# The output projection by pairs of token tiles, seven half-size products for eight, with sums on GpSimd

## The chip, the cores and the metric

The kernel runs on one core of a Trainium2 chip. The metric is the device time of one execution in microseconds. All arithmetic is fp32.

## The reference, cut to what matters

Two layers of an encoder run over 1152 token rows: 1024 of a prompt, and 8 x 16 of samples. Three branches (RWKV-7, latent attention, stick-breaking attention) each give 512 channels a row. At the end of a layer they are merged, projected and added to the residual:

```python
merged = (gA * ((yA * jax.nn.silu(zA)) @ P['w_br_rwkv'][l])
          + gB * ((yB * jax.nn.silu(zB)) @ P['w_br_mla'][l])
          + gC * ((yC * jax.nn.silu(zC)) @ P['w_br_sb'][l]))
x = x + gate * (merged @ P['w_out'][l])      # (1152 x 1024) @ (1024 x 1024)
```

The change touches the last line: `merged @ w_out`, and how its result gets into x.

## The kernel before

Each layer is a row of stages with a barrier between two (`Stages.stage`, line 116). The last one is `merge`. Each engine has its own program in it, and semaphores tie them together.

**Units.** 24 units (token half tp, branch b, pair of column blocks m) make the merged activations `M` (`mergedT`: channels on the partitions, 8 blocks x 1152 tokens). A unit is 14 products: 7 of the gate projection (four matmul steps of 288 columns each) and 7 of the branch projection (two steps each). Each group of 7 does a 2 x 2 block product by the scheme with seven multiplications, for which sums of blocks are made first: `quarter_sums` on GpSimd for the weights (line 2412), lines 2512 to 2515 on GpSimd for y, `h_sum` on VectorE for the normed input hT. ScalarE copies a partial bank (`kept`), VectorE adds it to another (`added`), and TensorE waits for the copy before it goes on accumulating in the same bank. VectorE adds each quarter to `M` and counts `merged`, one a unit.

**Output projection (lines 2571 to 2584).** `ups` lists 18 products: column half n of w_out, and token tile i of nine, half 0 first. Each is 8 matmul steps (128 x 128 weights from `M`, 512 columns of w_out) into one of four banks. The first two may start while VectorE ends the last unit, since they read only tokens of the first half; the third waits for `tanh_done`, and the fifth for all of `merged`. Each reuse of a bank waits for `update_read`. The halves of w_out lie where hT was (`w_half`); the second is loaded as the last unit's gate products end (line 2486).

**Update (lines 2660 to 2666).** For each product VectorE multiplies the bank by `gate` into t, tells `update_read`, and adds t to one of four x tiles. SP (the queue that issues DMAs) stores the tile, and loads the x tile for the update three places ahead into the one that came free. `InOrder` (line 94) makes an engine wait for the end of each of its own operations before the next. GpSimd has nothing to do in the stage once it has made the sums of the last unit.

Of the kernel before, what the change touches and what calls it, by code (L numbers as in the profile page):

```python
# [8 lines left out]
ALU = mybir.AluOpType  # L9
# [4 lines left out]
P = 128  # L14
D = 1024
KD = D // P
# [6 lines left out]
NT = T // P  # L23
# [2397 lines left out]
def merge(nc, S, A, l, ps, con, hT, yg, gates, x_in, x_out, wg0, wgs0):  # L2421
# [4 lines left out]
             "products", "kept", "tanh_done", "added", "quarter_read", "merged", "w_out0_loaded", "w_out1_loaded", "gate_loaded",  # L2426
             "x0_moved", "x1_moved", "x2_moved", "x3_moved", "updates", "update_read", "updated", "vec", "pool_own")
    with S.stage(*names) as (block, sb, (y0_loaded, y1_loaded, wg0_loaded, wg1_loaded, wb0_loaded, wb1_loaded, gate_sums, branch_sums, y_sums, h_sums,
                                         products, kept, tanh_done, added, quarter_read, merged, w_out0_loaded, w_out1_loaded, gate_loaded,
                                         x0_moved, x1_moved, x2_moved, x3_moved, updates, update_read, updated, vec, pool_own)):  # L2430
        M = sb("mergedT", [P, KD, T])
# [17 lines left out]
        NU, PER_Y = len(units), KD // 2  # L2449
        ups = [(n, i) for n in range(2) for i in range(NT)]  # L2450

# [45 lines left out]
        def _(pool):  # L2497
# [3 lines left out]
            for u in range(NU):  # L2501
# [15 lines left out]
                quarter_sums(G, own, wb[u % 2], wbs[u % 2], HP // 2, branch_sums)  # L2517

        @block.tensor
        def _(pe):  # L2520
# [49 lines left out]

            banks = (6, 7, 0, 1)
            pe.wait_ge(merged, NU // 2)
            for j, (n, i) in enumerate(ups):
                if i == 0:
                    pe.wait_ge(w_out_loaded[n], 16)
                if j == 2:
                    pe.wait_ge(tanh_done, 4 * NU)
                if j == 4:
                    pe.wait_ge(merged, NU)
                if j >= 4:  # L2580
                    pe.wait_ge(update_read, j - 3)
                for k in range(KD):
                    last = mm(ps[:, banks[j % 4], :], M[:, k, P * i:P * i + P], w_half(n)[:, k, :], start=(k == 0), stop=(k == KD - 1))  # L2583
                last.then_inc(updates, 1)

        @block.scalar
        def _(act):
# [10 lines left out]
            for u in range(NU):  # L2598
                keep(u, 1, gk[:, 0, :], 0)
                keep(u, 3, gk[:, 1, :], 0)  # L2600
                tanh(u, 0)
                keep(u, 4, gk[:, 2, :], 2)
                tanh(u, 1)
                tanh(u, 2)
                act.wait_ge(products, 14 * u + 7)
                if u >= 1:
                    act.wait_ge(quarter_read, u)
                do(gq[:, 3, :], ps[:, 0, 0:TQ], ACT.Tanh, scale=0.5).then_inc(tanh_done, 1)
                if u >= 1:
                    act.wait_ge(added, 6 * u)  # L2610
                keep(u, 8, bk[:, 0, :], 3)
                keep(u, 10, bk[:, 1, :], 3)
                keep(u, 11, bk[:, 2, :], 5)

        @block.vector
        def _(dve):
# [43 lines left out]
            put = InOrder(dve, updated)  # L2660
            for j, (n, i) in enumerate(ups):
                dve.wait_ge(updates, j + 1)
                dve.wait_ge(x_moved[j % 4], 16 * (2 * (j // 4) + 1))
                put(V.tensor_tensor(t[j % 2][:, :], ps[:, (6, 7, 0, 1)[j % 4], :], gate[:, int(i == NPT), 512 * n:512 * n + 512], ALU.mult))
                V.engine_nop().then_inc(update_read, 1)
                put(V.tensor_tensor(x[j % 4][:, :], x[j % 4][:, :], t[j % 2][:, :], ALU.add))


# [94 lines left out]
```

## Time and profile before

| | |
|---|---|
| median of 3 runs | 4752.07 us (4747.45 to 4758.35) |
| profiled execution | 4753.94 us, its span 4752.1 us |
| TensorE (PE) busy | 4376.5 us, 92% of the span |
| VectorE (DVE) busy | 2227.1 us, 47% |
| ScalarE (ACT) busy | 1628.7 us, 34% |
| GpSimd (POOL) busy | 731.5 us, 15% |
| line 2583, output projection, TensorE busy | 247.5 us in 576 records, for both layers |
| mean granted clock of TensorE | 0.969 of full speed |

The span runs from the first to the last instruction of one execution. Busy shares are means over stages with different limits, so what a stage is bound by is read in its own stretch. PE stands for matmuls, PEld for weight loads, which lie beside matmuls. The output projection of layer 0 lies from 2258.8 to 2382.5 us, that of layer 1 from 4623.9 to 4747.6 us. An fp32 matmul leaves two records in the trace.

### The profile page before, as it was taken

The numbers are of one execution on the slowest core, as the hardware profiler recorded it, in microseconds if no ns is written. First come the engines' busy times: TensorE is split into PE (matmuls) and PEld (weight loads), VectorE is DVE, ScalarE is ACT, GpSimd is POOL, SyncE is SP. The second block draws the span as 40 slices with busy tenths as digits, with TensorE's granted clock in tenths as the row PEclk, the third lists the DMA queues.
The fourth block names the chain that finished last, engine by engine and source line by source line (L and its number), as shares of the span: only waits on it lengthen the run. The fifth ranks groups of instructions, "written<-read, shape, count | busy, mean of one in ns | idle before, by whom it ended". The sixth has DMA issues, their size and how long they took to land. (4 is left out here: it accounts for less than half of the span.)

```text
span 4752.1 us, 74863 instructions
## 1 busy us (share of the span) xinstructions
PE 4376.5 (92%) x29552; PEld 3029.9 (64%) x29552; DVE 2227.1 (47%) x4660; ACT 1628.7 (34%) x3862; POOL 731.5 (15%) x940
## 2 busy tenths in 40 slices
PE   7899997988989989999979999979898999899999
PEld 3656665667666667777446666646666566677774
DVE  2555664345524453534225656633455244544341
ACT  4333333345523342112043333334455244411210
POOL 0011010000010015543000110000000100245430
PEclk9999998999999999999989999989999999999999
DMA  5010112010021122322241210120100211223222
GB/s 193 23 34 10 26 29 78 21 35 14 12 86 56 53 74 83 115 88 75 75 189 23 34 15 26 25 86 13 35 16 10 86 57 56 74 90 107 87 80 71
DMA packets 150654, 280.78 MB, mean 59 GB/s; under 512 B 51545, under 2 KB 77401, under 8 KB 145058
## 3 DMA queue, kind: packets, MB, share of 16 engines
q1 hardware_dynamic: 150306, 275.99, 18.2%
q8 instruction: 237, 3.88, 0.4%
q14 instruction: 111, 0.91, 0.1%
HBM read 230.96 MB, written 42.62 MB: 58 GB/s over the span
## 5 line engine op out<-in xcount | busy, mean ns | idle before, releaser
L1054 PE MATMUL banks<-hT,w_piece 128*128 128x384 f32 x1536 | 547.6, 498 | 6.3 <-ACT raw L1158 6.0
L1054 PEld LDWEIGHTS banks<-hT,w_piece 128*128 128x128 f32 x1536 | 280.6, 194 | 175.3 <-issue 14.0
L2232 PE MATMUL banks<-hT,w_piece 128*128 128x384 f32 x1056 | 354.1, 489 | 1.4 <-ACT sb_gate_raw L2342 1.4
L2232 PEld LDWEIGHTS banks<-hT,w_piece 128*128 128x128 f32 x1056 | 196.1, 190 | 141.4 <-issue 16.6
L2583 PE MATMUL banks<-hT,mergedT 128*128 128x512 f32 x576 | 247.5, 592 | 0.0
L1998 DVE SCALAR_TENSOR_TENSOR keysT<-banks,gains,rstd 64x128 f32<-64x128 f32 (+1 forms) x272 | 112.1, 412 | 249.1 <-ACT rstd L1912 246.6
L2592 ACT ACTIVATE gate_kept<-banks 128x288 f32<-128x288 f32 x144 | 59.0, 410 | 433.1 <-PE banks L2524 433.1
L2629 DVE TENSOR_TENSOR gate_quarters<-gate_kept,banks 128x288 f32<-128x288 f32 x144 | 65.4, 454 | 302.7 <-PE banks L2524 297.7
L2583 PEld LDWEIGHTS banks<-hT,mergedT 128*128 128x128 f32 x576 | 109.4, 190 | 137.0 <-issue 136.8
L2404 DVE TENSOR_TENSOR_SCAN left<-pass,zero 128x384 f32<-128x384 f32 (+7 forms) x144 | 189.8, 1318 | 5.0
L2629 DVE TENSOR_TENSOR branch_quarters<-branch_kept,banks 128x288 f32<-128x288 f32 x144 | 65.5, 455 | 270.3 <-PE banks L2524 270.3
L2401 DVE TENSOR_TENSOR pass<-pass,constants 128x128 f32<-128x128 f32 x128 | 41.5, 324 | 310.8 <-ACT take L2353 308.3
L1015 POOL TENSOR_TENSOR state_decayed<-state,decay_of_chunk 128x128 f32<-128x128 f32 x120 | 85.9, 716 | 572.7 <-DVE state L1287 568.9
L2524 PE MATMUL banks<-hT,w_gate_ahead 128*128 128x288 f32 x576 | 151.9, 415 | 7.4 <-PEq L132 7.4
L1830 PE MATMUL banks<-keysT,queriesT 96*128 96x512 f32 (+3 forms) x384 | 148.8, 496 | 8.7 <-DVE queriesT L1998 8.7
L2524 PE MATMUL banks<-y_branch,w_branch 128*128 128x288 f32 x576 | 155.3, 406 | 0.0
L2524 PE MATMUL banks<-hT,w_gate 128*128 128x288 f32 x576 | 147.5, 406 | 0.0
L2524 PEld LDWEIGHTS banks<-hT,w_gate_ahead 128*128 128x128 f32 x576 | 111.8, 195 | 40.0 <-issue 8.8
L1928 ACT ACTIVATE exponentials<-banks,maximum 128x384 f32<-128x384 f32 (+4 forms) x144 | 104.1, 723 | 92.8 <-DVE maximum L2011 91.2
L2229 PE MATMUL banks<-w_piece,hT 128*128 128x128 f32 x1152 | 132.7, 276 | 0.0
L1939 ACT ACTIVATE exponentialsT<-banks 128x512 f32<-128x512 f32 (+3 forms) x208 | 94.9, 488 | 105.3 <-PE banks L1842 104.7
L2229 PEld LDWEIGHTS banks<-w_piece,hT 128*128 128x128 f32 x1152 | 130.2, 192 | 1.0
(395 smaller groups left out, 9445.4 us busy)
## 6 DMA issues: line engine op xcount, KB each, us to landing
w_piece<-in_w_cols SPq DMA_DIRECT2D x66, 512.0 KB, 4.4
w_ada<-in_w_ada SPq DMA_DIRECT2D x24, 1024.0 KB, 9.4
w_gate_ahead<-in_w_cols SPq DMA_DIRECT2D x48, 512.0 KB, 4.3
w_branch<-in_w_br SPq DMA_DIRECT2D x96, 256.0 KB, 2.9
w_gate<-in_w_cols SPq DMA_DIRECT2D x48, 512.0 KB, 4.3
y_branch<-y_gated SPq DMA_DIRECT2D x12, 1152.0 KB, 8.2
sb_cached_keysT<-in_sbkT SPq DMA_DIRECT2D x8, 1024.0 KB, 6.9
sb_cached_values<-in_sbv SPq DMA_DIRECT2D x8, 1024.0 KB, 5.2
```

Source lines behind the costliest of these rows:

```text
L1015: G.tensor_tensor(SD[:, :], ST[:, :], R.pend[h % 2][:, n + 1:n + 2].broadcast_to([P, P]), ALU.mult).then_inc(sd_made, 1)
L1054: last = mm(dst, w[0 if kind in ("k", "v") else 1][:, k, :], hT[:, k, c], start=(k == 0), stop=(k == KD - 1))
L1830: last = mm(ps[:, b0 + a // 512, 0:e - a], Q[hh][:, P * i:P * i + P], K[hh][:, a:e], start=True, stop=True)
L1928: do(E[u % 3][:, 0:width(u)], sbank(u)[:, 0:width(u)], ACT.Exp, bias=mx[:, u:u + 1], scale=scale, accum_out=rsum[:, u:u + 1]).then_inc(exp ...
L1939: do(ET[:, s % 4, units[u][3], 0:cnt, :].rearrange("p q n -> p (q n)"), ps[:, ring_bank(("t", u, g)), 0:P * cnt], Copy).then_inc(ring_free, 1)
L1998: ins = V.scalar_tensor_tensor(to[hh][0:64, c], ps[hc, bank[n], at], par[hc, gain:gain + 1], rs[x % 2][hc, at], ALU.mult, ALU.mult)
L2229: last = mm(ps[:, bank[n], P * q:P * q + P], hT[:, k, P * i:P * i + P], w_of[wn][:, k, :], start=(k == 0), stop=(k == KD - 1))
L2232: last = mm(ps[:, bank[n], 0:TG], w_of[wn][:, k, :], hT[:, k, TG * g:TG * g + TG], start=(k == 0), stop=(k == KD - 1))
L2404: own(V.tensor_tensor_scan(mine[:, 0:n][:, ::-1], G[k][:, 0:n][:, ::-1], zero[:, 0:1].broadcast_to([P, n]), 1.0, ALU.mult, ALU.add))
L2524: ins = mm(ps[:, bank, 0:TQ], w[:, k, :], b[:, k, :], start=(first and k == 0), stop=(k == half - 1), skip_group_check=True)
L2583: last = mm(ps[:, banks[j % 4], :], M[:, k, P * i:P * i + P], w_half(n)[:, k, :], start=(k == 0), stop=(k == KD - 1))
L2629: own(V.tensor_tensor(dst, src, ps[:, bank, 0:TQ], ALU.add), added)
```

## The change

Two products stay as they were, for token tile 0: (0,0) and (1,0), eight steps each, one for each half of w_out. The other eight token tiles are taken in four pairs (`row_pair`). For a pair the rows are cut in two (one tile each), the inner dimension in two (4 blocks of 128 each), and the columns in two (512 each). The 2 x 2 block product is made in 7 products of four steps where there were 8, in the order of the units above.

The sums that it needs are made on GpSimd. For w_out there are four operations once a layer on [128, 4 x 512] elements: three go into buffers that the last units leave (`BS`: y_branch0, w_gate_ahead and w_gate1), and one over b12 in place, once the two whole products have read it (`updates` 2). For the pairs there is `quarter_sums` on [128, 4 x 128] elements, four operations a pair, into the buffers of the gate weights' sums and over a21 in `M`. ScalarE copies three partial banks a pair into the y_branch1 buffer (`ok`). VectorE adds them to a bank into t, and then multiplies and adds as before; the fourth update of a pair comes straight from its bank. Pairs take banks 0 to 2 and 3 to 5 in turn. Both halves of w_out are now needed for the first two products, and all of `merged` for the third. The order of the updates (`ups`), and with it that of the x tiles, is new. The semaphore names in the stage's list change with it: update_read goes, and out_products, out_kept, out_added, out_row_sums and out_sums come.

```diff
@@ -2447,7 +2447,14 @@
         w_out_loaded, x_moved = (w_out0_loaded, w_out1_loaded), (x0_moved, x1_moved, x2_moved, x3_moved)
         units = [(tp, b, m) for tp in range(2) for b in range(3) for m in range(KD // 2)]
         NU, PER_Y = len(units), KD // 2
-        ups = [(n, i) for n in range(2) for i in range(NT)]
+        NX = NPT // 2
+        ups = [(0, 0), (1, 0), *(u for x in range(NX) for u in ((0, 2 * x + 1), (1, 2 * x + 2), (1, 2 * x + 1), (0, 2 * x + 2)))]
+        wide = lambda ap, pattern: ap.rearrange(pattern)[:, 0:4 * 512].rearrange("p (k n) -> p k n", k=4)
+        BS = [wide(Y[0][:, :, :], "p h t -> p (h t)"), wide(wg[0][:, :, :, :], "p q k n -> p (q k n)"), wide(wg[1][:, :, :, :], "p q k n -> p (q k n)")]
+        ok = Y[1][:, :, :].rearrange("p h t -> p (h t)")[:, 0:3 * 512].rearrange("p (j n) -> p j n", j=3)
+
+        def row_pair(x):
+            return M[:, :, P * (2 * x + 1):P * (2 * x + 3)].rearrange("p k (q n) -> p q k n", q=2)
 
         def cols(tp, q):
             return slice(THALF * tp + TQ * q, THALF * tp + TQ * q + TQ)
@@ -2516,6 +2523,26 @@
                 pool.wait_ge(wb_loaded[u % 2], 32 * (u // 2 + 1))
                 quarter_sums(G, own, wb[u % 2], wbs[u % 2], HP // 2, branch_sums)
 
+            def row_sums(x):
+                if x >= 2:
+                    pool.wait_ge(out_products, 7 * (x - 1))
+                quarter_sums(G, own, row_pair(x), wgs[x % 2], KD // 2, out_row_sums)
+
+            pool.wait_ge(merged, NU // 2)
+            pool.wait_ge(products, 14 * (NU - 1) + 7)
+            row_sums(0)
+            for n in range(2):
+                pool.wait_ge(w_out_loaded[n], 16)
+            b11, b12, b21, b22 = (w_half(j)[:, KD // 2 * i:KD // 2 * i + KD // 2, :] for i in range(2) for j in range(2))
+            own(G.tensor_tensor(BS[0], b12, b11, ALU.subtract))
+            own(G.tensor_tensor(BS[1], b22, BS[0], ALU.subtract), out_sums)
+            own(G.tensor_tensor(BS[2], b21, BS[1], ALU.subtract))
+            pool.wait_ge(updates, 2)
+            own(G.tensor_tensor(b12, b22, b12, ALU.subtract), out_sums)
+            pool.wait_ge(merged, NU)
+            for x in range(1, NX):
+                row_sums(x)
+
         @block.tensor
         def _(pe):
             def product(bank, w, b, first, last):
@@ -2568,20 +2595,40 @@
                 pe.wait_ge(added, 6 * u + 5)
                 product(3, w[:, 1, half:HP], Ys[:, 2], False, True)
 
-            banks = (6, 7, 0, 1)
             pe.wait_ge(merged, NU // 2)
-            for j, (n, i) in enumerate(ups):
-                if i == 0:
-                    pe.wait_ge(w_out_loaded[n], 16)
-                if j == 2:
-                    pe.wait_ge(tanh_done, 4 * NU)
-                if j == 4:
+            for n in range(2):
+                pe.wait_ge(w_out_loaded[n], 16)
+                for k in range(KD):
+                    last = mm(ps[:, 6 + n, :], M[:, k, 0:P], w_half(n)[:, k, :], start=(k == 0), stop=(k == KD - 1))
+                last.then_inc(updates, 1)
+
+            def out_product(bank, w, b, first, last):
+                for k in range(KD // 2):
+                    ins = mm(ps[:, bank, :], w[:, k, :], b[:, k, :], start=(first and k == 0), stop=(k == KD // 2 - 1), skip_group_check=True)
+                ins.then_inc(out_products, 1)
+
+            half = KD // 2
+            b11, b12, b21, b22 = (w_half(j)[:, half * i:half * i + half, :] for i in range(2) for j in range(2))
+            for x in range(NX):
+                w, s, b0 = row_pair(x), wgs[x % 2], 3 * (x % 2)
+                if x == 0:
                     pe.wait_ge(merged, NU)
-                if j >= 4:
-                    pe.wait_ge(update_read, j - 3)
-                for k in range(KD):
-                    last = mm(ps[:, banks[j % 4], :], M[:, k, P * i:P * i + P], w_half(n)[:, k, :], start=(k == 0), stop=(k == KD - 1))
-                last.then_inc(updates, 1)
+                if x >= 2:
+                    pe.wait_ge(out_added, 4 * (x - 1))
+                out_product(b0, w[:, 0, 0:half], b11, True, False)
+                out_product(b0 + 1, w[:, 0, half:KD], b21, True, True)
+                pe.wait_ge(out_row_sums, x + 1)
+                pe.wait_ge(out_sums, 1)
+                pe.wait_ge(out_kept, 3 * x + 1)
+                out_product(b0, s[:, 1], BS[1], False, False)
+                out_product(b0 + 2, s[:, 0], BS[0], True, False)
+                pe.wait_ge(out_sums, 2)
+                pe.wait_ge(out_kept, 3 * x + 2)
+                out_product(b0, w[:, 1, 0:half], b12, False, False)
+                pe.wait_ge(out_kept, 3 * x + 3)
+                out_product(b0 + 2, s[:, 2], b22, False, True)
+                pe.wait_ge(out_added, 4 * x + 2)
+                out_product(b0, w[:, 1, half:KD], BS[2], False, True)
 
         @block.scalar
         def _(act):
@@ -2611,6 +2658,18 @@
                 keep(u, 8, bk[:, 0, :], 3)
                 keep(u, 10, bk[:, 1, :], 3)
                 keep(u, 11, bk[:, 2, :], 5)
+
+            def out_keep(x, n, j, read):
+                act.wait_ge(out_products, 7 * x + n)
+                if x >= 1:
+                    act.wait_ge(out_added, 4 * (x - 1) + read)
+                do(ok[:, j, :], ps[:, 3 * (x % 2) + (0, 0, 2)[j], :], ACT.Copy).then_inc(out_kept, 1)
+
+            act.wait_ge(products, 14 * NU)
+            for x in range(NX):
+                out_keep(x, 1, 0, 1)
+                out_keep(x, 3, 1, 3)
+                out_keep(x, 4, 2, 2)
 
         @block.vector
         def _(dve):
@@ -2658,12 +2717,26 @@
             dve.wait_ge(gate_loaded, 16)
             own(V.tensor_scalar(gate[:, :, :], gate[:, :, :], 0.5, None, ALU.mult))
             put = InOrder(dve, updated)
-            for j, (n, i) in enumerate(ups):
-                dve.wait_ge(updates, j + 1)
+
+            def update(j, source, read=None):
+                n, i = ups[j]
+                put(V.tensor_tensor(t[j % 2][:, :], source, gate[:, int(i == NPT), 512 * n:512 * n + 512], ALU.mult))
+                if read is not None:
+                    own(V.engine_nop(), read)
                 dve.wait_ge(x_moved[j % 4], 16 * (2 * (j // 4) + 1))
-                put(V.tensor_tensor(t[j % 2][:, :], ps[:, (6, 7, 0, 1)[j % 4], :], gate[:, int(i == NPT), 512 * n:512 * n + 512], ALU.mult))
-                V.engine_nop().then_inc(update_read, 1)
                 put(V.tensor_tensor(x[j % 4][:, :], x[j % 4][:, :], t[j % 2][:, :], ALU.add))
+
+            for n in range(2):
+                dve.wait_ge(updates, n + 1)
+                update(n, ps[:, 6 + n, :])
+            for x_ in range(NX):
+                for j, (n, kept_n, slot, bank) in enumerate(((2, 1, 0, 1), (5, 3, 2, 0), (6, 2, 1, 2))):
+                    dve.wait_ge(out_products, 7 * x_ + n)
+                    dve.wait_ge(out_kept, 3 * x_ + kept_n)
+                    own(V.tensor_tensor(t[j % 2][:, :], ok[:, slot, :], ps[:, 3 * (x_ % 2) + bank, :], ALU.add), out_added)
+                    update(2 + 4 * x_ + j, t[j % 2][:, :])
+                dve.wait_ge(out_products, 7 * x_ + 7)
+                update(2 + 4 * x_ + 3, ps[:, 3 * (x_ % 2), :], out_added)
 
 
 def pieces(w):
```

## Rows read from the trace of the kernel before

**Rows 1.** the page: span, and busy time of TensorE (its share is in brackets)

```profile
span 4752.1 us, 74863 instructions
...
PE 4376.5 (92%) x29552; PEld 3029.9 (64%) x29552; DVE 2227.1 (47%) x4660; ACT 1628.7 (34%) x3862; POOL 731.5 (15%) x940
```

**Rows 2.** chain that ended last, in order of time: start us, us, what, times

```profile
4579.89 44.13 PE banks L2524 x182
4624.03 123.61 PE banks L2583 x288
```

**Rows 3.** the page's costliest groups: busy, mean ns of one, idle before

```profile
L2583 PE MATMUL banks<-hT,mergedT 128*128 128x512 f32 x576 | 247.5, 592 | 0.0
...
L2583 PEld LDWEIGHTS banks<-hT,mergedT 128*128 128x128 f32 x576 | 109.4, 190 | 137.0 <-issue 136.8
```

**Rows 4.** line 2583 by stretch: us, PE, PEld busy, granted clock, DMA, GB/s

```profile
2258.76:2382.52 123.76, 123.76 (x288) 54.53 (x287) 1.00 0.21 69
4623.86:4747.60 123.74, 123.73 (x288) 54.53 (x287) 1.00 0.21 70
```

**Rows 5.** instructions in order of time, layer 0: start us, us, engine, line

```profile
2250.03 2.10 PE L2524 MATMUL banks<-h_sums,w_gate 128*128 128x288 f32 x8
...
2251.97 2.10 PE L2524 MATMUL banks<-y_branch,w_branch 128*128 128x288 f32 x8
...
2252.16 0.60 SPq L2486 DMA_DIRECT2D hT<-in_w_out  x1
...
2258.76 123.76 PE L2583 MATMUL banks<-hT,mergedT 128*128 128x512 f32 x288
```

**Rows 6.** line 2486: both loads of the second half of w_out, issue to landing

```profile
DMA to landing us min/median/max: 8.5/8.8/9.1
```

**Rows 7.** instructions in order of time, layer 1: load, first output product

```profile
4617.27 0.60 SPq L2486 DMA_DIRECT2D hT<-in_w_out  x1
...
4623.86 4.46 PE L2583 MATMUL banks<-hT,mergedT 128*128 128x512 f32 x10
```

**Rows 8.** GpSimd by line: duration ns min/median/max, first and last start

```profile
L2415 POOL TENSOR_TENSOR w_gate_sums_ahead<-w_gate_ahead x24: 1261/1268/1273, 1403.4 to 4561.1; 128x512 f32<-128x512 f32 x24
...
L1011 POOL TENSOR_TENSOR silu_z<-silu_z,temp x8: 2616/2618/2630, 228.2 to 3093.7; 128x1152 f32<-128x1152 f32 x8
...
L1020 POOL TENSOR_TENSOR bonus<-r_shifted,v_transposed x8: 2989/2996/3090, 151.4 to 3019.6; 128x1152 f32<-128x1152 f32 x8
```

**Rows 9.** instructions in order of time: VectorE beside GpSimd's sums, layer 0

```profile
2156.50 1.27 POOL L2416 TENSOR_TENSOR w_gate_sums_ahead<-w_gate_sums_ahead,w_gate_ahead 128x512 f32<-128x512 f32 x1
...
2156.68 1.40 DVE L2638 SCALAR_TENSOR_TENSOR gate_quarters<-gate_quarters,branch_quarters 128x288 f32<-128x288 f32 x1
...
2157.85 1.37 POOL L2417 TENSOR_TENSOR w_gate_ahead<-w_gate_ahead 128x512 f32<-128x512 f32 x1
...
2158.12 1.42 DVE L2639 TENSOR_TENSOR mergedT<-mergedT,gate_quarters 128x288 f32<-128x288 f32 x1
```

**Rows 10.** instructions in order of time: VectorE around the first output product

```profile
2254.65 0.46 DVE L2638 SCALAR_TENSOR_TENSOR gate_quarters<-gate_quarters,branch_quarters 128x288 f32<-128x288 f32 x1
...
2257.07 0.45 DVE L2629 TENSOR_TENSOR branch_quarters<-branch_kept,banks 128x288 f32<-128x288 f32 x1 [1.47 <-PE banks L2524]
...
2260.99 0.46 DVE L2639 TENSOR_TENSOR mergedT<-mergedT,gate_quarters 128x288 f32<-128x288 f32 x1
...
2261.49 1.22 DVE L2659 TENSOR_SCALAR gate<-gate 128x2048 f32<-128x2048 f32 x1
```

**Rows 11.** groups of instructions: copies of 512 columns, and the update's multiplication

```profile
L1939 ACT ACTIVATE exponentialsT<-banks 128x512 f32<-128x512 f32 x96 | 55.6, 596 | 82.5 <-PE banks L1842 82.5
...
L2664 DVE TENSOR_TENSOR update<-banks,gate 128x512 f32<-128x512 f32 x18 | 12.5, 692 | 95.7 <-PE banks L2583 95.7
```

**Rows 12.** DMA issues, layer 0's projection: KB each, median us to landing

```profile
x_rows<-in_x_prompt SPq DMA_DIRECT2D x12, 256.0 KB, 3.0
```

**Rows 13.** by stretch: us, busy PE, PEld, DVE, ACT, POOL, clock, DMA, GB/s

```profile
2382.60:2400.00 17.40, 0.00 (x0) 0.00 (x0) 1.61 (x4) 5.63 (x9) 0.00 (x0) 0.56 0.71 271
```

More of the change, by code:

```diff
@@ L2426, in merge @@
              "products", "kept", "tanh_done", "added", "quarter_read", "merged", "w_out0_loaded", "w_out1_loaded", "gate_loaded",
-             "x0_moved", "x1_moved", "x2_moved", "x3_moved", "updates", "update_read", "updated", "vec", "pool_own")
+             "x0_moved", "x1_moved", "x2_moved", "x3_moved", "updates", "updated", "out_products", "out_kept", "out_added", "out_row_sums", "out_sums", "vec", "pool_own")
     with S.stage(*names) as (block, sb, (y0_loaded, y1_loaded, wg0_loaded, wg1_loaded, wb0_loaded, wb1_loaded, gate_sums, branch_sums, y_sums, h_sums,
                                          products, kept, tanh_done, added, quarter_read, merged, w_out0_loaded, w_out1_loaded, gate_loaded,
-                                         x0_moved, x1_moved, x2_moved, x3_moved, updates, update_read, updated, vec, pool_own)):
+                                         x0_moved, x1_moved, x2_moved, x3_moved, updates, updated, out_products, out_kept, out_added, out_row_sums, out_sums, vec, pool_own)):
         M = sb("mergedT", [P, KD, T])
```

## The prediction

> **What bounds the kernel now.** I read the page first: TensorE is busy for 92% of the span, and no other engine for more than half of that share [rows 1]. An average says nothing of one stage, so the chain that ended last comes next. It shows that in the last stretch the matmuls of line 2524 run into those of line 2583 without a gap, and that line 2583 then holds the chain for 123.6 us, until the last residual update [rows 2]. The group of line 2583 has no idle time ahead of it [rows 3], and its two stretches, one for each layer, are 123.76 and 123.74 us of PE busy without a hole, at a granted clock of 1.00, the upper of the two levels (2.4 GHz) [rows 4]. So the output projection costs what its matmuls cost, and nothing else in that stretch sets its end. The next layer begins behind a barrier, and so what is saved in layer 0 moves all that follows.
>
> **What is removed.** A layer has 18 products (nine tiles, two column halves) of eight steps: 144 matmuls. In the trace each is two records, 288 a layer. 123.76 us / 144 = 0.859 us for a matmul [rows 4]. After the change it is 2 products of eight steps and 4 pairs x 7 products x 4 steps: 16 + 112 = 128 matmuls. Sixteen fewer, of the same shape (128 rows of weights, 512 columns): 16 x 0.859 = 13.75 us a layer, 27.5 us in all. All of it lies on the path.
>
> **Shorter products.** The new products wait between each four steps, where the old ones waited between each eight. The gate products of line 2524 have this form (four steps, semaphores between, accumulation into a bank that ScalarE copies meanwhile). One takes 1.94 us from its start to that of the next (2250.03 to 2251.97) [rows 5], which is 242.5 ns a record at 288 columns. A record at 512 columns takes 123.76 / 288 = 429.7 ns. The difference, 187.2 ns for 224 columns, is 0.836 ns a column, two cycles at 2.4 GHz (0.833), so nothing is left over. So a boundary whose waits are already met costs nothing that shows: I take 0. The upper bound is one exposed weight load, 0.19 us [rows 3], at each of 28 boundaries: 5.3 us a layer.
>
> **When the operands are needed (layer 0).** The first output product starts at 2258.76 [rows 5]. With 0.859 us a matmul: product (0,0) ends at 2265.6, (1,0) at 2272.5. Then the seven of pair 0, 3.44 us each, end at 2275.9, 2279.4, 2282.8, 2286.3, 2289.7, 2293.1, 2296.6. So the second half of w_out is needed at 2265.6 (before: only after nine tiles), `merged` in full at 2272.5 (before: at the fifth product, 2286.3), the first wide sums (`out_sums` 1) at 2279.4, and the last (`out_sums` 2) at 2286.3.
>
> **The second half of w_out.** Its load was issued at 2252.16, as the gate products ended [rows 5]. The two such loads landed 8.5 to 9.1 us after issue [rows 6], so at 2260.7 to 2261.3, 4.3 us before the need. In layer 1: issued at 4617.27, landed by 4626.4, needed at 4623.86 + 6.87 = 4630.7 [rows 6, 7]. Nothing in front of it in SP's queue changes but which four x tiles are loaded. Cost 0; without that cover it would be PE's stall one to one.
>
> **GpSimd's sums.** The trace has no operation on 2048 elements. Its nearest are 1.27 us for 512 and 2.62 or 3.00 us for 1152 elements [rows 8]. Carried on in a line: (2.62 - 1.27) / 640 = 2.11 ns an element, so 2.62 + 896 x 2.11 = 4.5 us; the steeper line, (3.00 - 1.27) / 640 = 2.7 ns, gives 5.4 us. I take 4.5, since the operations of the cheap row and of the 512 row are of the same plain kind, and keep 5.4 as the upper end. The first `row_sums` (four operations of 1.27 to 1.37 us as in [rows 9], and the gaps) runs from 2252.2 to 2257.9. The wide ones start as w_out lands: from 2260.7, at 4.6 each with the gap, they end at 2265.3, 2269.9, 2274.5 and 2279.1. The fourth overwrites a block that (1,0) reads, and waits for the end of that, 2272.5, which has passed. `out_sums` 1 has 9.5 us to spare, `out_sums` 2 7.2 us; at 5.5 each it is 2282.7 and 3.6 us. Row sums of pair 1 end at 2284.8, needed only at 2303; those of pairs 2 and 3 wait for pairs 0 and 1 to end, 5.7 us of work with a pair's length of cover. Cost 0.
> The Trainium skill ("GPSIMD Engine Reference", section "3.1 Elementwise — side-by-side cycle accounting") gives 4497 ns for this very operation at 2048 elements. By it the sum is unchanged, and no run here shows it yet.
>
> **VectorE behind GpSimd.** Here the change adds a real wait. A VectorE operation with two inputs in SBUF that starts inside a GpSimd operation ends only 0.3 us after that one: at 2156.68 the 0.46 us operation took 1.40 us, the next one 1.42 us [rows 9]. GpSimd itself lost 0.1 us. Until now this met operations of 256 to 576 elements, and now it meets some of 4.5 us. Step by step: the first row sums lie beside the operations at 2254.65 and just after it. Two in a row ended 2.86 us after the first one's start in [rows 9]; here that is 2257.5, against the addition due at 2257.07 [rows 10] for which the unit's last product waits. So 0 to 0.4 us a layer; placed on the grid of GpSimd's starts (2254.9 to 2256.3) the second ends at 2256.6, so 0. The last `mergedT` addition starts at 2260.99 [rows 10]. Caught behind the first wide sum it ends at 2265.6; caught once more at 2270.2; the need is 2272.5. Behind it the gate's scaling (1.2 us, 2261.49 [rows 10]) and the first two x additions are each caught once at most: scaling done by 2271.1, update 0 by 2274.8, update 1 by 2279.4, update 2 by 2282.4. The next addition from which TensorE waits is due at 2289.7, and so has 7 us of cover. Cost 0.
> The Trainium skill ("SBUF — State Buffer", section "SBUF: two separate sides") calls the pair an exclusive lock: whichever starts first "gets the pair for the whole instruction". The trace agrees [rows 9]. By it this wait grows with the length of GpSimd's operation, which speaks against the change; what it would cost is the second rival below.
>
> **ScalarE and VectorE within a pair.** A copy of 512 columns from a bank is 0.6 us, an operation of VectorE on 512 columns 0.69 us [rows 11]. Each copy has a whole product, 3.44 us, before its bank is written again. VectorE does 11 operations a pair, 7.6 us in 24; the densest place is an addition, a multiplication and an x addition (2.1 us) between products 5, 6 and 7, 3.44 us apart. TensorE's last product waits for the addition behind product 5, 0.7 of 3.44 us. The multiplications for three of four updates read SBUF twice and can be caught behind row sums, 1.4 us; the addition that TensorE needs reads a bank and isn't. Cost 0.
>
> **x tiles.** Updates now come in bursts, but three of them never take less than four products, 13.7 us. A load is issued once the update three places ahead is done, and lands in 3.0 us [rows 12]. Cost 0. The last update is again one tile from a bank, an addition and a store: the tail stays.
>
> **Sum.** 4752.1 - 2 x 13.75 = 4724.6 us of span; the profiled execution took 4753.9, 1.8 us around the span, which gives 4726.4. The median of the three runs is 1.9 us below the profiled one, so the forecast for a median is 4724.6 us, 0.6% less.
>
> **Rivals.**
> (a) Boundaries cost. If every four-step product exposed a weight load, 2 x 5.3 us come back: 4735. For it: twice as many semaphore waits. Against it: the 1.94 us of the gate products.
> (b) VectorE is caught more often. If three wide sums in a row each held an operation of the last unit's chain, `merged` would come at 2275.2 (at 5.4 us each, 2277.4) and not 2272.5: 2.7 to 4.9 us a layer, 4730 to 4734. It needs w_out to land by 2259.5, in 7.3 us; the shortest load seen is 8.5.
> (c) The wide sums are late in part. Above (2286.3 - 2260.7) / 4 = 6.4 us each, product 5 waits for the fourth; at 8 us by 6.7 us a layer: 4738.
> (d) The other side. The same wait, but with sums so slow that it eats more than the matmuls give: that is from (2286.3 + 13.75 - 2260.7) / 4 = 9.8 us each. At 12 us the stall is 22.4, the loss 8.7 us a layer: 4769. TensorE's clock would add to it: in the 17 us without matmuls after the last product the granted clock averages 0.56 [rows 13], so matmuls after a stall could run at the lower level (1.2 GHz). For it: the width was never run here, and rows of M are read in pieces of 128. Against it: the dearest row, carried on, ends at 5.4.
> (e) The matmuls are fewer but something outside, such as run to run scatter or another placement, hides it: 4743 to 4761.
>
> **How the numbers follow.** Forecast 0.78; (a) 0.05, (b) 0.04, (c) 0.05, (e) 0.05, (d) 0.03. A measurement of this kernel tells about 0.2%, 9.5 us, from no change, so faster means below 4742.6: 0.92. Same 0.05, slower 0.03. The forecast alone holds about 4720 to 4730. The range takes in (a) and (b) and some scatter of the runs (4747 to 4758 before): 4718 to 4736.
>
> **What would show it.** Right: 256 records a layer for the output projection, in one piece of 110.0 us with no idle time of TensorE; wide sums of 4.5 us; the last `mergedT` addition and the gate's scaling stretched to about 4.5 us, with nobody waiting. Wrong: TensorE idle ahead of the third or fifth product of pair 0, put down to GpSimd (c, d); ahead of the first, put down to VectorE (b); idle of 0.2 us at many boundaries (a); wide sums above 6.4 us.

## The result and the profile after

| | before | changed |
|---|---|---|
| median | 4750.62 us (4 runs, 4747.45 to 4758.35) | 4717.31 us (4 runs, 4712.1 to 4724.06) |
| ratio, with its 95% interval | | 0.9933 (0.9917 to 0.9949) |
| profiled execution, its span | 4753.94 us, 4752.1 us | 4724.06 us, 4722.2 us |
| same comparison with more runs (below, `again`) | 4747.24 us (24 runs) | 4721.71 us (6 runs), ratio 0.9946 (0.9931 to 0.9961) |

The forecast was 4724.6 us, a ratio of 0.9942 for 27.5 us. Both intervals hold that ratio. Against the stated range of 4718 to 4736 us, the first median of 4717.31 lies 0.7 us below its lower end, and the median with more runs, 4721.71, within it. Both are under the 4742.6 us that the prediction took as the line for faster.

The page of the changed kernel, against [rows 1]: TensorE is busy for 34 us less, with 64 records less. 27.5 us of that are the projections; the other 6 us lie in stages that the change doesn't touch.

```profile
span 4722.2 us, 74875 instructions
...
PE 4342.7 (92%) x29488; PEld 3013.1 (64%) x29488; DVE 2275.1 (48%) x4684; ACT 1644.4 (35%) x3886; POOL 813.5 (17%) x980
```

The end of the chain that ended last (start us, us, what). Where [rows 2] had one piece of line 2583, there are now the two whole products (line 2602) and the four pairs (line 2607), again without a gap:

```profile
4569.94 37.80 PE banks L2551 x155
4607.74 13.73 PE banks L2602 x32
4621.47 96.15 PE banks L2607 x224
```

Busy time of TensorE in the two projections, from the start of the first matmul to the end of the last (us, PE busy, PEclk, DMA share, GB/s), against [rows 4]:

```profile
2254.11:2364.11 110.00, 110.00 (x257) 1.00 0.24 78
4607.50:4717.60 110.10, 110.10 (x257) 1.00 0.23 77
```

110.0 us a layer where it was 123.76, at the same granted clock of 1.00. From the start of the first matmul to the end of the last it is 123.76 and 110.04 us in both layers, so the 13.75 us are there to within 0.03 us. (257 records are 256 and one that reaches into the stretch; the second stretch begins 0.07 us before its first output matmul, which starts at 4607.57.) In order of time (start us, us, engine, line), the same first products in layer 0:

```profile
2254.11 13.90 PE L2602 MATMUL banks<-hT,mergedT 128*128 128x512 f32 x32
...
2267.85 7.03 PE L2607 MATMUL banks<-hT,mergedT 128*128 128x512 f32 x16
...
2274.72 3.60 PE L2607 MATMUL banks<-w_gate_ahead,w_gate_sums_ahead 128*128 128x512 f32 x8
...
2278.15 3.60 PE L2607 MATMUL banks<-y_branch,w_gate_sums_ahead 128*128 128x512 f32 x8
...
2281.58 3.60 PE L2607 MATMUL banks<-hT,mergedT 128*128 128x512 f32 x8
...
2285.01 3.60 PE L2607 MATMUL banks<-hT,w_gate_sums_ahead 128*128 128x512 f32 x8
...
2288.45 3.60 PE L2607 MATMUL banks<-w_gate,mergedT 128*128 128x512 f32 x8
...
2291.88 7.03 PE L2607 MATMUL banks<-hT,mergedT 128*128 128x512 f32 x16
```

The products of pair 0 start 3.43 us apart: a four-step product after a wait costs what four steps cost. `x16` is two products of one operand pair that the view has merged.

The load of the second half of w_out, against [rows 6] (two loads):

```profile
DMA to landing us min/median/max: 9.2/9.2/9.2
```

And GpSimd with VectorE beside it, layer 0, against [rows 9] and [rows 10]:

```profile
2256.35 0.46 DVE L2698 TENSOR_TENSOR mergedT<-mergedT,gate_quarters 128x288 f32<-128x288 f32 x1
...
2256.83 4.50 POOL L2537 TENSOR_TENSOR y_branch<-hT 128x2048 f32<-128x2048 f32 x1 [3.67 <-DMA hT<-in_w_out]
2256.85 5.56 DVE L2718 TENSOR_SCALAR gate<-gate 128x2048 f32<-128x2048 f32 x1
...
2261.41 5.38 POOL L2538 TENSOR_TENSOR w_gate_ahead<-hT,y_branch 128x2048 f32<-128x2048 f32 x1
...
2263.18 4.16 DVE L2727 TENSOR_TENSOR x_rows<-x_rows,update 128x512 f32<-128x512 f32 x1
...
2266.87 4.85 POOL L2539 TENSOR_TENSOR w_gate<-hT,w_gate_ahead 128x2048 f32<-128x2048 f32 x1
...
2268.84 3.42 DVE L2727 TENSOR_TENSOR x_rows<-x_rows,update 128x512 f32<-128x512 f32 x1
...
2271.79 4.84 POOL L2541 TENSOR_TENSOR hT<-hT 128x2048 f32<-128x2048 f32 x1
...
2275.69 1.50 DVE L2723 TENSOR_TENSOR update<-update,gate 128x512 f32<-128x512 f32 x1
```

Each wide sum takes 4.50 us when it starts alone (line 2537) and 4.84 to 5.38 behind a caught VectorE operation. VectorE's gate scaling, 1.22 us before [rows 10], is 5.56 us; its x additions, 0.69 us [rows 11], are 4.16 and 3.42 us. TensorE has no idle time in this stretch for any of it.

### The profile page after: what moved, and what is told of

It reads as the page before. It is cut to its first block and busy times, and to the rows that moved or that the text cites. A ratio compares the mean times of both kernels' runs of the same rounds, so it can differ in the third digit from the quotient of the medians.

```text
span 4722.2 us, 74875 instructions
## 1 busy us (share of the span) xinstructions
PE 4342.7 (92%) x29488; PEld 3013.1 (64%) x29488; DVE 2275.1 (48%) x4684; ACT 1644.4 (35%) x3886; POOL 813.5 (17%) x980
## 5 line engine op out<-in xcount | busy, mean ns | idle before, releaser
L1830 PE MATMUL banks<-keysT,queriesT 96*128 96x512 f32 (+3 forms) x384 | 148.8, 496 | 8.7 <-DVE queriesT L1998 8.7
L2212 POOL TENSOR_TENSOR sb_outT<-sb_outT,sb_gate 128x128 f32<-128x128 f32 x72 | 34.8, 484 | 576.9 <-ACT sb_outT L2374 575.8
L2643 ACT ACTIVATE gate_quarters<-gate_quarters 128x288 f32<-128x288 f32 x144 | 63.5, 441 | 194.2 <-DVE gate_quarters L2688 193.6
```

The source lines that it names most:

```text
L1830: last = mm(ps[:, b0 + a // 512, 0:e - a], Q[hh][:, P * i:P * i + P], K[hh][:, a:e], start=True, stop=True)
```

## Theories and experiments

**Theory M**: only the number of matmuls counts. The sums lie wholly beside them, four-step boundaries cost nothing, and where the sums stop being hidden can be reckoned from the cover that the prediction gives (the time by which an operand is ready ahead of its need). **Rival X**: the reordered updates, or something outside the projection, give part of the gain, since the first medians are 33 us apart and not 27.5. **Rival S**: the sums do cost something that the waits don't show. **Rival L**: the cover is other than reckoned, so the kernel is nearer to a stall, or further.

To tell these apart a run's time isn't enough. In one kernel's runs the time moves by up to 29 us with the mean granted clock of TensorE (before: 4737 us at 0.974, 4766 us at 0.966). So the table gives three things: the comparison of times; the stretch from layer 1's first output product to the end of the span, which holds nothing but the projection; and the time at a mean clock of 0.970, from a least squares fit over the 126 runs of the table with one slope for all kernels (3.5 us for 0.001 of clock; 95% about 1 to 3 us). Each ratio is to runs of the kernel before that were made beside that kernel, in three groups with medians of 4747.2, 4752.7 and 4754.6 us; with an offset for each group in the fit, the distance between before and changed is 24.5 us instead of 24.3. Where an edit makes TensorE wait, the mean clock falls too (0.964 in `sums_thrice`, 0.971 in the changed kernel), and the last column understates the price.

| kernel | runs | ratio to before (95%) | projection to end, layer 1 | at clock 0.970 |
|---|---|---|---|---|
| before | 52 | | 128.2 us | 4749.4 |
| changed (first runs and `again`) | 10 | 0.9933 (0.9917 to 0.9949), 0.9946 (0.9931 to 0.9961) | 114.6 | 4725.1 |
| eight_products | 12 | 1.0007 (0.9998 to 1.0017) | 128.4 | 4752.1 |
| no_sums | 7 | 0.9965 (0.9952 to 0.9979) | 114.6 | 4726.7 |
| sums_on_vector | 6 | 0.9943 (0.9923 to 0.9963) | 114.6 | 4723.8 |
| gate_in_unit_1 | 6 | 0.9937 (0.9918 to 0.9956) | 114.6 | 4724.6 |
| late_w_out | 5 | 0.9949 (0.9934 to 0.9964) | 117.3 | 4729.4 |
| sums_plus_two | 4 | 0.9955 (0.9938 to 0.9972) | 120.5 | 4733.4 |
| sums_twice | 10 | 1.0006 (0.9995 to 1.0017) | 131.3 | 4750.3 |
| gate_first | 10 | 0.9989 (0.9976 to 1.0003) | 114.6 | 4741.6 |
| sums_thrice | 4 | 1.0091 (1.0069 to 1.0113) | 148.8 | 4770.5 |

### again: the changed kernel in more rounds

No edit.

> The changed kernel once more, in more rounds. Theory M (only the 32 matmuls that are gone count, 27.5 us): ratio 0.9942. Rival X (the reordered updates, or something outside the projection, give another 5 to 6 us): ratio 0.993 or below, and the stretches outside the two projections shorter than before in this trace as well, by the same amounts and in the same layers as in the first pair of traces (layer 0 up to the projection 4.7 us shorter, from one projection to the next 2.1 us longer). M expects these amounts to come out otherwise.

Measured: 0.9946 (0.9931 to 0.9961), which is 25.6 us of 4747. In the trace layer 0's projection starts at 2250.84; it was 2258.76 before and 2254.11 in the first trace of the changed kernel, though no instruction ahead of the merge stage differs. From one projection's start to the next it is 2350.55 us, and 2353.46 in the first trace. The amounts outside came out otherwise, so they are scatter, not the change.

### eight_products: everything but the seven-product scheme

```diff
-                out_product(b0, w[:, 0, 0:half], b11, True, False)
-                out_product(b0 + 1, w[:, 0, half:KD], b21, True, True)
...
+                for j, (q, n) in enumerate(((0, 0), (1, 1), (0, 0), (1, 1), (0, 1), (1, 0), (0, 1), (1, 0))):
+                    i = j // 2 % 2
+                    if i:
+                        pe.wait_ge(out_kept, 4 * x + 2 * (j // 4) + j % 2 + 1)
+                    out_product(b0 + 2 * (j // 4) + j % 2, w[:, q, half * i:half * i + half], w_half(n)[:, half * i:half * i + half, :], i == 0, i == 1)
```

A pair has four banks, ScalarE copies each at half its sum, and VectorE updates each straight from its bank.

> The change without the seven-product scheme: tiles in pairs, updates in the new order, both halves of w_out needed at once, four-step products with a copy by ScalarE and a wait between, but eight of them a pair, and no sums. 144 matmuls a layer as before. Theory M: as long as the kernel before, ratio 1.000 (0.999 to 1.001), 288 records of 429.7 ns a layer without idle time. Rival X: about 5 us shorter than before, ratio 0.999 or less. Rival of the boundaries (a): up to 10 us longer, 1.002.

Measured: 1.0007 (0.9998 to 1.0017). Its matmuls in layer 0's projection (busy us, mean ns of one, idle before):

```profile
L2587 PE MATMUL banks<-hT,mergedT 128*128 128x512 f32 x256 | 110.0, 592 | 0.0
L2582 PE MATMUL banks<-hT,mergedT 128*128 128x512 f32 x32 | 13.9, 592 | 0.0
```

Idle time 0.0 ahead of 256 records in four-step products with waits between. 110.0 us / 256 is 429.7 ns a record, as before. So rival (a) of the prediction is out, and so is X: the new order of updates and x tiles alone gains nothing. If anything the kernel is 2.7 us longer at equal clock, a little more than the fit's error of 1.6 us for that distance. Both its projections take 123.76 us, as before, and behind the last matmul of layer 1 it takes 0.15 us more. Where the rest would lie, no trace shows.

### no_sums: GpSimd's sums left out

```diff
-                pe.wait_ge(out_row_sums, x + 1)
-                pe.wait_ge(out_sums, 1)
...
-            for x in range(1, NX):
-                row_sums(x)
```

> GpSimd's sums for the output projection (row sums and wide sums) are left out with the waits on them, so that the seven products multiply whatever lies in the buffers; the output of the projection is not the reference's. Theory M (sums wholly hidden): the same time as the changed kernel, within 0.1%. If the sums cost something, in VectorE's waits or TensorE's operands, this is shorter than the changed kernel by that.

Measured: ratio 0.9965 (0.9952 to 0.9979), a median of 4732.5 us, so longer than the changed kernel and not shorter. The reason is not in the projection, which takes 114.6 us to the end as in the changed kernel, and 110.0 in layer 0 (first line: stretch, us, busy PE, PEld, DVE, ACT, POOL, PEclk, DMA share, GB/s). The second line is a stretch of layer 1's latent attention. The last block has one group of matmuls of that stage, first in this trace, then in that of `again`:

```profile
2245.54:2355.54 110.00, 110.00 (x257) 48.45 (x255) 35.53 (x53) 7.16 (x12) 0.00 (x0) 1.00 0.23 77
...
3631.00:3646.00 15.00, 12.97 (x60) 6.34 (x53) 8.27 (x25) 4.63 (x14) 0.91 (x2) 0.69 0.04 14
```

```profile
3636.61 3.75 PE L1830 MATMUL banks<-keysT,queriesT 96*128 96x512 f32 x4 [2.03 <-DVE queriesT L1998]
```

```profile
3632.88 1.96 PE L1830 MATMUL banks<-keysT,queriesT 96*128 96x512 f32 x4 [2.02 <-DVE queriesT L1998]
```

The same four records, behind the same idle time of 2.0 us, took 3.75 us here and 1.96 us there. The mean granted clock of the 15 us around them was 0.69 here (part of it at the lower level, 1.2 GHz), and 1.00 there (2.4 GHz). From the end of one projection to the start of the next this trace spent 11 to 14 us more than those of the changed kernel. At equal clock the two kernels are 1.6 us apart, within the error. So the sums cost nothing in the projection, which speaks against S, but the run's time alone would have misled. Why the clock was lower over the seven runs (mean 0.968, where the changed kernel had 0.971) stays open: layer 1 computes with other values here, and the phase of everything after layer 0 is other too.

### sums_on_vector: the wide sums on the other engine

```diff
-            own(G.tensor_tensor(BS[0], b12, b11, ALU.subtract))
...
+            own(V.tensor_tensor(BS[0], b12, b11, ALU.subtract))
```

> The four wide sums are made by VectorE instead of GpSimd, the first three ahead of its first update, the fourth behind its second. From VectorE's 1.36 us for 1152 elements: 2.3 us each, so three end at about 2263.8, updates 0 and 1 are at most 2.8 us late, the fourth ends at about 2272. Nobody waits: the same time as the changed kernel within 0.1%. If it is faster, the exclusive use of the port by GpSimd cost something after all.

Measured: 0.9943 (0.9923 to 0.9963), the same as the changed kernel, and no idle time of TensorE in either projection. The durations were a miss:

```profile
2255.65 3.24 DVE L2724 TENSOR_TENSOR y_branch<-hT 128x2048 f32<-128x2048 f32 x1
...
2256.82 3.19 POOL L2416 TENSOR_TENSOR w_gate_sums<-w_gate_sums,mergedT 128x512 f32<-128x512 f32 x1
...
2258.92 3.24 DVE L2725 TENSOR_TENSOR w_gate_ahead<-hT,y_branch 128x2048 f32<-128x2048 f32 x1
...
2268.59 2.29 DVE L2730 TENSOR_TENSOR hT<-hT 128x2048 f32<-128x2048 f32 x1
```

3.24 us each and not 2.3, since GpSimd's row sums (1.3 us alone) took turns with them and were stretched to 3.2 themselves; the fourth, with GpSimd idle, took 2.29. So the two engines took turns, whichever had the wide operation. One turn of both took 3.27 us (2255.65 to 2258.92), 0.3 us less than 2.29 and 1.27 us together. The third wide sum ended 13.8 us after the first output product had started (2251.66), where the expectation had 9.7 (2263.8 less 2254.11 of its scale): 4.1 us late, 1.3 of them because the scaling stood in front, and still with nobody waiting.

### gate_first and gate_in_unit_1: the gate's scaling out of GpSimd's way

```diff
+            dve.wait_ge(gate_loaded, 16)
+            own(V.tensor_scalar(gate[:, :, :], gate[:, :, :], 0.5, None, ALU.mult))
             h_sum(0)
```

> VectorE scales the gate at the start of the stage instead of between the last unit and the first update. The second wide sum, 5.38 us in the changed kernel beside this operation, goes back to about 4.5 us, the end of the fourth wide sum comes about 0.9 us earlier, and the time stays the same within 0.1%, since nobody waits for either. If the 5.38 us have another cause (the x addition beside it), they stay.

Measured: 0.9989 (0.9976 to 1.0003), a median of 4744.6 us, where the changed kernel's time was expected. The cause is the edit's own place (line waited for: us, times, longest):

```profile
PE banks L2551 <- DVE h_sums L2681: 11.7, 1, 11.7
```

The gate's load stands in SP's queue behind that of the first y, so at the head of the stage VectorE waited for it ahead of `h_sums`, and TensorE for those: 11.7 us in layer 0, and 12.1 in layer 1. The 24 units of a layer took 510.8 and 512.4 us, where the other traces have 496.6 to 499.8. What the run was made for did come out (instruction in order of time, layer 0): the second wide sum is back to

```profile
2272.80 4.61 POOL L2538 TENSOR_TENSOR w_gate_ahead<-hT,y_branch 128x2048 f32<-128x2048 f32 x1
```

To show that the wait for the load was all, the scaling was moved to unit 1:

```diff
+                if u == 1:
+                    dve.wait_ge(gate_loaded, 16)
+                    own(V.tensor_scalar(gate[:, :, :], gate[:, :, :], 0.5, None, ALU.mult))
                 add(u, 2, 1, gq[:, 0, :], gk[:, 0, :], 1)
```

> As gate_first, but the scaling stands in unit 1, where the gate has long landed, so that h_sums is not held up. If the 12 to 13 us a layer by which gate_first was longer were the wait for the gate's load ahead of h_sums, they are gone, and the kernel takes as long as the changed one within 0.1%. The second wide sum takes about 4.6 us, not 5.4. If VectorE's order at the end of the stage had to do with them, they stay.

Measured: 0.9937 (0.9918 to 0.9956), units at 499.4 and 498.8 us, the second wide sum 4.60 us, the projection 114.6 us. So VectorE's order there is free, and 0.8 us of GpSimd's 5.38 came from the scaling.

### sums_plus_two, sums_twice, sums_thrice: where the sums stop being hidden

```diff
-            own(G.tensor_tensor(BS[2], b21, BS[1], ALU.subtract))
+            for _ in range(3):
+                own(G.tensor_tensor(BS[2], b21, BS[1], ALU.subtract))
```

This is `sums_plus_two`. In `sums_twice` the first and second sum are made twice as well (`sums_thrice`: three, three and five times):

```diff
-            own(G.tensor_tensor(BS[0], b12, b11, ALU.subtract))
-            own(G.tensor_tensor(BS[1], b22, BS[0], ALU.subtract), out_sums)
+            for _ in range(2):
+                own(G.tensor_tensor(BS[0], b12, b11, ALU.subtract))
+            for r in range(2):
+                own(G.tensor_tensor(BS[1], b22, BS[0], ALU.subtract), out_sums if r == 1 else None)
```

> The third wide sum is made three times: two operations of about 4.85 us more in front of the fourth. In the changed kernel the fourth ended at 2276.6, 5.0 us before the fifth product wanted it (2281.6). Prediction's reckoning of the cover: 2 x 4.9 - 5.0, TensorE idle about 4.8 us ahead of the fifth product of pair 0, nothing ahead of the third; about 9.6 us in all over the changed kernel. If the cover were really larger or smaller than 5 us, the idle time is 9.8 us less that.

Who waited for whom on TensorE, layer 0 (us, times, longest), and the stalled product with the one after it:

```profile
PE banks L2608 <- POOL hT L2542: 4.6, 1, 4.6
```

```profile
2279.00 5.40 PE L2608 MATMUL banks<-hT,mergedT 128*128 128x512 f32 x8 [4.61 <-POOL hT L2542]
...
2284.23 3.60 PE L2608 MATMUL banks<-hT,w_gate_sums_ahead 128*128 128x512 f32 x8
```

Expected 4.8 us of idle time, measured 4.6 in layer 0 and 4.0 in layer 1. The two more operations took 9.8 and 10.4 us, so the cover was 5.2 and 6.4 us, where the trace of the changed kernel gives 5.0 and 5.1. In layer 0 the wide sums started 0.3 us sooner than there; in layer 1 they started 0.4 us sooner, and the second of them took 4.60 us instead of 5.37. With that the covers agree within 0.2 us, and rival L is out. The expected price in time was short, though. The stretch to the end is 120.5 us, 5.9 more than 114.6, for 4.0 us of idle time. The rest is the stalled product itself: 5.40 us in the row, where 3.60 is usual. The mean granted clock of those 5.40 us was 0.68 in layer 0, and 1.00 again behind them.

> Every wide sum is made twice, the third one three times, eight operations in all on 2048 elements. From the trace of the changed kernel, layer 0: first one at 2256.8, about 4.9 us each; the first pair's third product would wait from 2274.7 to about 2276, its fifth until the eighth ends at about 2295.5, where it would start at 2281.6. Stall 13.9 us a layer, 27.8 us in all: about 4745, so all that the matmuls gave is lost again; up to 4752 if TensorE's clock falls to the lower level in the gap. If the sums were further from the path than the prediction says, less.

```profile
PE banks L2610 <- POOL hT L2544: 11.8, 1, 11.8
PE banks L2610 <- issue: 1.7, 1, 1.7
```

```profile
2258.95 9.77 POOL L2540 TENSOR_TENSOR w_gate_ahead<-hT,y_branch 128x2048 f32<-128x2048 f32 x2
...
2268.82 3.67 PE L2610 MATMUL banks<-w_gate_ahead,w_gate_sums_ahead 128*128 128x512 f32 x8 [1.69 <-issue]
...
2283.20 4.49 POOL L2544 TENSOR_TENSOR hT<-hT 128x2048 f32<-128x2048 f32 x1
...
2287.75 6.25 PE L2610 MATMUL banks<-hT,mergedT 128*128 128x512 f32 x8 [11.83 <-POOL hT L2544]
...
2293.83 3.60 PE L2610 MATMUL banks<-hT,w_gate_sums_ahead 128*128 128x512 f32 x8
```

The fifth product started at 2287.75, 41.4 us after the first output product; the expectation had 2295.5, which is 41.4 us too. The profile names no releaser for the 1.7 us (`issue`), but the second copy of the second sum ended at 2268.72, and the product started at 2268.82. The stall was 1.7 us ahead of the third and 11.8 ahead of the fifth product (13.5, expected 13.9). The product behind the long one then took 6.25 us at a mean granted clock of 0.59, while the one behind the short one took 3.67, as good as the usual 3.60. Layer 1, with idle times of 1.8 and 11.8 us, lost 16.7 (131.3 less 114.6). Ratio 1.0006 (0.9995 to 1.0017): what the matmuls gave is gone, as reckoned.

> Twelve wide operations: each sum three times, the third one five times. Third product of pair 0 waits 10.9 us, the fifth another 22.5 us, 33.4 us a layer: about 4784 without loss of clock, up to 4800 with it. This is rival (d), the other side of the prediction: slower than the kernel before.

```profile
PE banks L2610 <- POOL hT L2544: 17.7, 1, 17.7
PE banks L2610 <- issue: 10.9, 1, 10.9
```

28.6 us of idle time in layer 0 (29.9 in layer 1) where 33.4 was expected: the wait ahead of the third product was met (10.9), and the one ahead of the fifth was put 4.8 us too high (17.7 for 22.5). The third product, stalled, took 6.61 us instead of 3.60, and GpSimd's sums ran on beside it, so 3.0 us of the expected second wait went into that product. Most of the rest is that the sums took 4.8 us each and not 4.9. Layer 1 lost 34.2 us (148.8 less 114.6). Ratio 1.0091 (1.0069 to 1.0113), 4790 us: rival (d) of the prediction, brought about. Its trace also shows the catch that the prediction had for the last `mergedT` addition and that the changed kernel just missed:

```profile
2254.29 9.18 POOL L2538 TENSOR_TENSOR y_branch<-hT 128x2048 f32<-128x2048 f32 x2 [3.13 <-DMA hT<-in_w_out]
2254.33 4.77 DVE L2701 TENSOR_TENSOR mergedT<-mergedT,gate_quarters 128x288 f32<-128x288 f32 x1
```

The addition came 0.04 us behind GpSimd's start and took 4.77 us. In the changed kernel (row at 2256.35 above) it had ended 0.02 us before.

### late_w_out: the load's cover

```diff
-            sp.wait_ge(products, 14 * (NU - 1) + 7)
+            sp.wait_ge(products, 14 * NU)
             sp.dma_start(w_half(1), A["w_out"][l, :, :, 512:D]).then_inc(w_out_loaded[1], 16)
```

> The second half of w_out is loaded 6.8 us later, behind the last branch product instead of the last gate product. Prediction's reckoning: issued at about 2254.1 (scale of the changed kernel's trace), landed at 2262.6 to 2263.2, needed at 2261.0: TensorE idle 1.6 to 2.2 us ahead of product (1,0) in each layer, 3 to 4.5 us in all. The wide sums move too, by 6.3 us, and the fourth then ends at about 2283, where the fifth product wants it at 2283.2 to 2283.8: no stall there. If the cover was larger than reckoned, the same time as the changed kernel.

```profile
2245.50 0.59 SPq L2493 DMA_DIRECT2D hT<-in_w_out  x1
...
2254.35 7.13 PE L2602 MATMUL banks<-hT,mergedT 128*128 128x512 f32 x16 [2.01 <-DMA hT<-in_w_out]
```

Product (1,0) started at 2254.35 instead of 2252.18: 2.0 us of idle time in layer 0 and 2.3 in layer 1 (expected 1.6 to 2.2), and 2.6 us more to the end of the span. No stall at the fifth product, as expected. Ratio 0.9949 (0.9934 to 0.9964): so small a stall isn't seen in the ratio, only in the trace. The eight-step product behind it took 7.13 us, where 16 records side by side usually take 7.03: behind this idle time hardly anything was lost on top.

## Why the prediction was right, point by point

- **Removed matmuls.** 16 a layer at 0.859 us: 123.76 to 110.04 us, in both layers, and `eight_products` puts the steps back and has the old time. Right, and it is the whole of the sum.
- **Boundaries, bounded at 5.3 us a layer, taken as 0.** Right: 3.43 us from product to product, and no idle time in `eight_products`.
- **w_out's load.** It landed 9.2 us after issue, a little over the rows' 8.5 to 9.1, and 4.3 to 4.4 us before the need (taken: 4.3). Right; `late_w_out` shows that the reckoning holds when the cover is taken away.
- **Wide sums at 4.5 us, upper bound 5.4.** Single ones are 4.50 and 4.55. The term mis-sized is their train: four were put at 18.4 us, and took 19.8 (2256.83 to 2276.63). "GpSimd itself lost 0.1 us" was read from VectorE operations of 0.46 us; the longer ones here cost it 0.3 to 0.9 us each. With the later start the fourth ended 5.0 us ahead of its need, and not 7.2 us. Hidden all the same.
- **VectorE caught behind GpSimd.** The kind was right and the count one too high: the scaling and the two x additions were caught, the last `mergedT` addition missed it by 0.02 us. The Trainium skill ("SBUF — State Buffer", section "SBUF: two separate sides") calls the port pair that the two engines share an exclusive lock, held for a whole instruction; the rows agree: 5.56 us for a scaling of 1.22 that started 0.02 us behind a sum of 4.50, and 1.08 us behind its end. The first row sums met the last unit's addition: it took 1.41 us, and TensorE didn't wait:

```profile
2250.36 1.36 POOL L2417 TENSOR_TENSOR mergedT<-mergedT 128x512 f32<-128x512 f32 x1
...
2250.63 1.41 DVE L2698 TENSOR_TENSOR mergedT<-mergedT,gate_quarters 128x288 f32<-128x288 f32 x1
...
2252.43 0.46 DVE L2688 TENSOR_TENSOR branch_quarters<-branch_kept,banks 128x288 f32<-128x288 f32 x1 [0.39 <-PE banks L2551]
```

- **Rival (d)'s price.** Break-even was put at a mean of 9.8 us for each of four sums. `sums_twice` has the work of 9.8 us each and lands at 1.0006. The mechanism and its place are shown. The loss of clock was named without a size; over eight stalls with idle times of 4.0 to 18.4 us it is 1.8 to 3.0 us a stall, and it doesn't grow with the idle time (3.0 behind 10.9, 2.0 behind 18.4). Two slips of the sums change nothing here: at 8 us a sum, rival (c)'s stall is 32 less 25.6, 6.4 us and not 6.7; and (b) reckons its sums from 2260.7, while its condition asks for a start at 2259.5.
- **Total.** 27.5 us forecast. The two comparisons give 31.8 (24 to 39) and 25.6 (19 to 33) us, and the profiled spans 29.9, of which 27.5 lie in the projections and 2.4 outside. That the first median came out 33 us under the kernel before, and so below the stated range, is most likely scatter: those four runs had mean clocks of 0.971 to 0.973, where the kernel before has 0.9695 over its 52. At equal mean clock the fit gives 24.3 us, 1.5 us less than its error of 1.7 allows for 27.5, and 27.0 against `eight_products`. Both would fit if the rearrangement that the two kernels share cost about 2.7 us outside the projections, but that isn't shown. What the difference is stays open; the stretches of the projections in the traces leave no room for it.

## What to carry to other kernels

Where one engine's work is an unbroken chain, the gain of removing work is its own duration, and what matters is the date by which each new operand is needed: write the dates down, and take the cover as their difference. A sum moved to an idle engine is free until its date. Beyond it each microsecond costs one, and each stall of 4 us or more cost 1.8 to 3.0 us on top here, since TensorE came back at a lower clock; stalls of 1.7 to 2.3 us in this stage cost 0.1 to 0.3. For a change of half a per cent compare the stretch that holds it in two traces: in the runs of one kernel the time moved by as much with the mean clock as the change gives.

## What the runs showed of the hardware that was not expected

- Most of the scatter between runs of one kernel goes with the mean granted clock of TensorE: 4737 us at 0.974 and 4766 at 0.966, 3.5 us for 0.001 in the fit over 126 runs. The kernel before scatters by 6.7 us (standard deviation), and the fit leaves 2.5.
- After an idle time of 4.0 or 4.6 us the next eight records took 5.40 us where 3.60 is usual, after 11.8 us 6.17 and 6.25, after 10.9 us 6.61, but after 18.4 us only 5.56. After 1.7 us they took 3.67. In another stage four records took 3.75 us in one trace and 1.96 in another, behind the same idle time of 2.0 us, so the idle time alone doesn't say what the clock does.
- GpSimd and VectorE operations with two inputs in SBUF take turns, and both pay: three VectorE operations on 2048 elements took 3.24 us each, where one alone took 2.29, and four GpSimd operations of 1.27 us took 2.19 to 3.20. The turn of both took 3.27 us, 0.3 less than the two alone.
